# Weights' low halves: all of them on VectorE, in two pieces a slot

## The chip, the cores and the metric

The kernel runs on one core of a Trainium2 chip. The metric is the device time of one execution in microseconds (us), the median of several runs. Inputs, weights and outputs are in fp32 and lie in the chip's main memory.

## The reference

A trunk of two layers works on two requests of 256 positions with 1024 features, with shared weights. Cut to what matters:

```python
def trunk(x, ...):
    for l in range(DEPTH):                       # 2 layers
        h = rmsnorm(x, g_mix[l])
        u_a, v_a, q, k, v_b, g_a, g_b = split(h @ w_in[l])
        y_a = spatial_gating(u_a, v_a, sgu_g[l], sgu_w[l], sgu_b[l])
        y_b = diff_attention(q, k, v_b, lam, lam_init, rel_bias, sub_g[l])
        br = einsum('nbsc,ncd->nbsd', stack([y_a, y_b]), w_br[l])
        merged = sigmoid(g_a) * br[0] + sigmoid(g_b) * br[1]
        x = x + merged @ w_out[l]
        x = x + conv_gated_mlp(rmsnorm(x, g_ffn[l]), w_up[l], conv_w[l], conv_b[l], w_down[l])
    return rmsnorm(x, g_final)
```

diff_attention has 8 heads with two softmax maps each; conv_gated_mlp is an up-projection to 2 x 2816 columns, a depthwise convolution of width 3, a gelu gate and a down-projection. Nearly all arithmetic is in the products with the weight matrices.

## The kernel before

**Slots.** Both requests lie side by side as 512 columns. The weight matrices are worked through in blocks of 1024 rows x 256 columns ("slots"), 74 a layer: 16 of q, k, v and va (S_R), 4 of u (S_U), 16 of gates and branches (S_M1, S_M2), 4 of w_out (S_O), 22 of w_up (S_F), 12 of w_down (S_D; 8 of these have seven rows of tiles, not eight). Slot s uses buffer s % 2 of raw, w_hi and w_lo. SyncE loads raw; ScalarE writes the high half w_hi as two copies, L480 for the first kd(s) of the eight tiles of 256 columns and L481 for the rest; the low half w_lo = raw - w_hi comes in two pieces too, the first from VectorE (L837, waits for the first copy), the rest from GpSimd (L416, waits for the second). kd(s) is 4 in slots 0 to 3, 1 in slots 4 to 19, 3 elsewhere, so the rest has 1024, 1792 or 1280 elements a partition (1024 where a slot has seven tiles). TensorE makes each product from three matmuls a tile, high x high (L1188), low x high (L1189) and high x low (L1190), for two halves of 128 columns; in the v and va slots these are L1223 to L1225. SyncE loads slot s+2 when both pieces of slot s are done.

**Queues.** Every engine's program is written out by hand and done in that order; semaphores tie the engines together. hi_split counts ScalarE's copies, lo_vector and lo_pool the pieces of w_lo.

**Attention rounds.** The projections of q, k, v, va and u are interleaved with the heads' attention in four rounds (r = 0 to 3) of eight steps (i = 0 to 7), two heads a round, one query tile a step. In step i TensorE does half a slot, then the values product of the tile two steps back (L1274, into the one bank HEAD), the transposition of attn of the last step, and the logits of two steps ahead (L1247). VectorE in step i: split of the coming slot if i is even; softmax_out (reciprocal L898, map_ratio L900, attn L905); at i = 6 and, from round 1 on, i = 2 head_scale (L911 and head_o L915), which empties the bank HEAD after a head's four tiles; at i = 0 and 4 head_lo (yb_lo L921); softmax_in of the next tile (L886, L890); at i = 1 to 4 the low parts of the next heads' q and k (L847); and the evacuation of TensorE's half slot (L864, L874 or L961). ScalarE in step i: squares of the head, at even i the two copies of the slot (L480, L481), the high parts of q or k (L547, L549), head_hi (L589), the transposed attn (L566), the exponentials (L556). GpSimd does half of the low parts of k (L426) beside its w_lo pieces, and the sums of squares of the norms (L401, L404).

The head values product must wait for head_o when it starts a new head:

```python
                if a % 4 == 0 and a:
                    pe.wait_ge(head_o_ok, l * HEADS + a // 4)
```

**After the rounds** spatial_gating (L968 on) works a 256-column block at a time: a split, the gates, another split, mix (L991, L998), ya_lo (L1002) and, once, the last head's yb_lo; the last head's branch product is L1373 to L1375. In the MLP, mlp(i) copies the conv parameters (L1054), splits two slots, evacuates four half slots (L1063) and convolves each (ScalarE L706, VectorE L1069 and L1072).

## Time and profile before

| | |
|---|---|
| median of 3 runs | 1741.06 us (1739.48 to 1742.98) |
| the profiled execution | 1740.8 us |
| its span, first to last instruction | 1738.8 us |
| TensorE's mean granted clock | 0.996 of full speed |
| TensorE busy | 98% of the span |
| VectorE, ScalarE, GpSimd busy | 55%, 43%, 33% |
| memory traffic | 101 GB/s on average |

The profile's page has busy times, a picture of the span in 40 slices and the costliest groups. Behind it stand views of the trace: who waited for whom, groups of instructions by line and shape, and the instructions in order of time. In the order of time a row is start in us, duration in us, engine and line, operation, output and inputs with partitions x elements, count, and in brackets the idle time before it with what ended it. Rows that follow one another closely are merged with a count. Instructions of one engine overlap by some 0.08 us, so the next one starts a little before the last has ended.

### The profile page before, as it was taken

The numbers are of one execution on the slowest core, as the hardware profiler recorded it, in microseconds if no ns is written. First come the engines' busy times: TensorE is split into PE (matmuls) and PEld (weight loads), VectorE is DVE, ScalarE is ACT, GpSimd is POOL, SyncE is SP. The second block draws the span as 40 slices with busy tenths as digits, with TensorE's granted clock in tenths as the row PEclk, the third lists the DMA queues.
The fourth block names the chain that finished last, engine by engine and source line by source line (L and its number), as shares of the span: only waits on it lengthen the run. The fifth ranks groups of instructions, "written<-read, shape, count | busy, mean of one in ns | idle before, by whom it ended". The sixth has DMA issues, their size and how long they took to land.

```text
span 1738.8 us, 21578 instructions
## 1 busy us (share of the span) xinstructions
PE 1708.6 (98%) x7950; PEld 1425.5 (82%) x7950; DVE 948.5 (55%) x1328; ACT 739.1 (43%) x1312; POOL 575.3 (33%) x216
## 2 busy tenths in 40 slices
PE   7999999999999999999999999999999999999997
PEld 5888888788888888888888888878888888888886
DVE  5677754543337777741147667545333477777122
ACT  5465654222344444432245656442223444443223
POOL 2544432322243222223344334223223432222332
PEclk8999999999999999999999999999999999999999
DMA  6422222222422222233253222322242232222332
GB/s 218 134 90 80 73 73 97 97 83 87 145 97 97 96 96 96 96 99 102 91 193 97 74 73 73 116 79 73 97 145 97 94 100 96 96 96 91 99 101 84
DMA packets 152303, 174.90 MB, mean 101 GB/s; under 512 B 2936, under 2 KB 141874, under 8 KB 151730
## 3 DMA queue, kind: packets, MB, share of 16 engines
q1 hardware_dynamic: 151328, 173.55, 30.2%
q10 hardware_dynamic: 914, 0.55, 0.2%
q8 instruction: 37, 0.61, 0.2%
q14 instruction: 24, 0.20, 0.0%
HBM read 167.78 MB, written 6.31 MB: 100 GB/s over the span
## 4 chain that ended last, share of the span: by engine, by line
PE 91%; DVE 5%; ACT 2%; issue 1%; ACTq 0%; DMA 0%; DVEq 0%
PE bank L1188 26%; PE bank L1190 26%; PE bank L1189 26%; PE bank L1223 3%; PE bank L1224 3%; PE bank L1225 3%; PE bank L1247 1%; PE bank L1274 1%; DVE attn L905 1%; DVE q_st L847 1%; PE bank L1346 1%; PE bank L1258 1%; DVE w_lo L837 0%; DMA table<-in_rel_bias 0%; DVE k_lo L847 0%
## 5 line engine op out<-in xcount | busy, mean ns | idle before, releaser
L416 POOL TENSOR_TENSOR w_lo<-raw,w_hi 128x1280 fp32r<-128x1280 f32 (+2 forms) x148 | 483.7, 3268 | 1085.0 <-ACT w_hi L481 1084.9
L1188 PE MATMUL bank<-xg_hi,w_hi 128*128 128x512 f32 x1344 | 527.2, 392 | 0.9 <-issue 0.9
L1190 PE MATMUL bank<-xg_hi,w_lo 128*128 128x512 f32 x1344 | 523.6, 390 | 0.0
L1189 PE MATMUL bank<-xg_lo,w_hi 128*128 128x512 f32 x1344 | 523.5, 390 | 0.0
L1188 PEld LDWEIGHTS bank<-xg_hi,w_hi 128*128 128x128 f32 x1344 | 252.8, 188 | 52.9 <-issue 2.3
L1190 PEld LDWEIGHTS bank<-xg_hi,w_lo 128*128 128x128 f32 x1344 | 252.6, 188 | 53.1
L1189 PEld LDWEIGHTS bank<-xg_lo,w_hi 128*128 128x128 f32 x1344 | 252.8, 188 | 51.9 <-issue 1.0
L837 DVE TENSOR_TENSOR w_lo<-raw,w_hi 128x768 fp32r<-128x768 f32 (+2 forms) x148 | 129.5, 875 | 193.5 <-ACT w_hi L480 193.3
L481 ACT ACTIVATE w_hi<-raw 128x1280 fp32r<-128x1280 f32 (+2 forms) x149 | 196.0, 1315 | 0.0
L480 ACT ACTIVATE w_hi<-raw 128x768 fp32r<-128x768 f32 (+2 forms) x149 | 112.5, 755 | 154.6 <-PE bank L1190 141.5
L1190 PE MATMUL bank<-g_hi,w_lo 128*128 128x512 f32 x352 | 136.9, 389 | 0.0
L1188 PE MATMUL bank<-g_hi,w_hi 128*128 128x512 f32 x352 | 136.9, 389 | 0.0
L1189 PE MATMUL bank<-g_lo,w_hi 128*128 128x512 f32 x352 | 136.9, 389 | 0.0
L706 ACT ACTIVATE conv<-up,conv_par 128x512 f32<-128x512 f32 x88 | 71.9, 817 | 146.8 <-DVE up L1063 146.8
L556 ACT ACTIVATE logit<-logit,neg_max 128x256 f32<-128x256 f32 x128 | 64.1, 502 | 128.7 <-DVE neg_max L890 128.4
L1063 DVE TENSOR_TENSOR up<-bank,rms 128x512 f32<-128x512 f32 x88 | 60.5, 687 | 75.0 <-PE bank L1190 56.0
L1223 PE MATMUL bank<-w_hi,xg_hi 128*128 128x512 f32 x256 | 100.4, 392 | 0.0
L1225 PE MATMUL bank<-w_lo,xg_hi 128*128 128x512 f32 x256 | 99.7, 389 | 0.0
L1224 PE MATMUL bank<-w_hi,xg_lo 128*128 128x512 f32 x256 | 99.6, 389 | 0.0
L1069 DVE SCALAR_TENSOR_TENSOR conv<-up,conv_par,conv 128x510 f32<-128x510 f32 x88 | 70.5, 801 | 53.3 <-ACT conv L706 53.2
L1188 PEld LDWEIGHTS bank<-g_hi,w_hi 128*128 128x128 f32 x352 | 66.1, 188 | 13.8
L1189 PEld LDWEIGHTS bank<-g_lo,w_hi 128*128 128x128 f32 x352 | 66.1, 188 | 13.7
(157 smaller groups left out, 2372.7 us busy)
## 6 DMA issues: line engine op xcount, KB each, us to landing
raw<-in_w_in SPq DMA_DIRECT2D x57, 1024.0 KB, 5.1
raw<-in_w_up SPq DMA_DIRECT2D x44, 1024.0 KB, 5.0
raw<-in_w_br SPq DMA_DIRECT2D x16, 1024.0 KB, 5.1
raw<-in_w_down SPq DMA_DIRECT2D x16, 896.0 KB, 4.7
raw<-in_w_out SPq DMA_DIRECT2D x8, 1024.0 KB, 5.1
raw<-in_w_down SPq DMA_DIRECT2D x8, 1024.0 KB, 5.1
x_spill<-x_res SPq DMA_DIRECT2D x2, 2048.0 KB, 7.6
x_res<-x_spill SPq DMA_DIRECT2D x2, 2048.0 KB, 9.6
```

The source lines that it names most:

```text
L416: nc.gpsimd.tensor_tensor(w_lo[p_][:, kd(s):n, :], raw[p_][:, kd(s):n, :], f32(w_hi[p_][:, kd(s):n, :]), ALU.subtract).then_inc(lo_pool, 1)
L480: nc.scalar.activation(w_hi[s % 2][:, 0:kd(s), :], raw[s % 2][:, 0:kd(s), :], ACT.Copy).then_inc(hi_split, 1)
L481: nc.scalar.activation(w_hi[s % 2][:, kd(s):n, :], raw[s % 2][:, kd(s):n, :], ACT.Copy).then_inc(hi_split, 1)
L706: nc.scalar.activation(conv[half][:, :, :], up[half][:, :, :], ACT.Identity, bias=conv_par[:, 3, ab, half:half + 1], scale=conv_par[:, 1, ...
L837: nc.vector.tensor_tensor(w_lo[p_][:, 0:kd(s), :], raw[p_][:, 0:kd(s), :], f32(w_hi[p_][:, 0:kd(s), :]), ALU.subtract).then_inc(lo_vector, 1)
L1069: nc.vector.scalar_tensor_tensor(c[:, :, 1:SEQ], u[:, :, 0:SEQ - 1], conv_par[:, 0, ab, half:half + 1], c[:, :, 1:SEQ], ALU.mult, ALU.add) ...
L1188: nc.tensor.matmul(out, w_hi[w][:, k, cols], x_hi[:, a, :], start=first and k == 0, stop=False)
L1189: nc.tensor.matmul(out, w_hi[w][:, k, cols], x_lo[:, a, :], start=False, stop=False)
L1190: mm = nc.tensor.matmul(out, w_lo[w][:, k, cols], x_hi[:, a, :], start=False, stop=last and k == kt - 1)
L1223: nc.tensor.matmul(bank[t][:, :], xg_hi[:, a, cols], wide_hi[:, k, :], start=first, stop=False)
L1224: nc.tensor.matmul(bank[t][:, :], xg_lo[:, a, cols], wide_hi[:, k, :], start=False, stop=False)
L1225: mm = nc.tensor.matmul(bank[t][:, :], xg_hi[:, a, cols], wide_lo[:, k, :], start=False, stop=last)
```

## The change

GpSimd's pieces of w_lo go to VectorE: split on VectorE now issues the first piece, waits for ScalarE's second copy, and issues the rest. The semaphore lo_pool is called lo_rest. On GpSimd only the low parts of k and the sums of squares are left, and its loops over slots are gone. What is computed is the same, as is kd(s). The program of TensorE, ScalarE and SyncE is the same but for the semaphore's name.

```diff
@@ -225,7 +225,7 @@
     raw_in = [sem(f"raw_in{i}") for i in range(2)]
     hi_split = sem("hi_split")
     lo_vector = sem("lo_vector")
-    lo_pool = sem("lo_pool")
+    lo_rest = sem("lo_rest")
     proj_done = sem("proj_done")
     evacuated = sem("evacuated")
     xg_hi_ok, xg_lo_ok = sem("xg_hi_ok"), sem("xg_lo_ok")
...
@@ -305,7 +305,7 @@
             def load(s, src, off=0, n=8):
 
                 sp.wait_ge(lo_vector, l * SLOTS + off + (s + 1))
-                sp.wait_ge(lo_pool, l * SLOTS + off + (s + 1))
+                sp.wait_ge(lo_rest, l * SLOTS + off + (s + 1))
                 sp.dma_start(raw[s % 2][:, 0:n, :], src).then_inc(raw_in[s % 2], 16)
 
             def block_of(w, col, kt=(0, 8)):
...
@@ -405,17 +405,8 @@
                       .then_inc(sum_ok, 1)
                 yield m
 
-        pool.wait_ge(hi_split, 2)
-        nc.gpsimd.tensor_tensor(w_lo[0][:, kd(0):, :], raw[0][:, kd(0):, :], f32(w_hi[0][:, kd(0):, :]), ALU.subtract)\
-          .then_inc(lo_pool, 1)
 
         for l in range(DEPTH):
-            def split(s, off=0, n=8):
-                p_ = s % 2
-                pool.wait_ge(hi_split, 2 * (l * SLOTS + off) + 2 * (s + 1))
-                nc.gpsimd.tensor_tensor(w_lo[p_][:, kd(s):n, :], raw[p_][:, kd(s):n, :], f32(w_hi[p_][:, kd(s):n, :]),
-                                        ALU.subtract).then_inc(lo_pool, 1)
-
             def k_parts(p, half):
 
                 t, hi, lo = qk_f32[half], k_hi[(2 * p + half) % 3], k_lo[(2 * p + half) % 3]
@@ -427,36 +418,13 @@
                       .then_inc(k_lo_pool, 1)
                     pool.wait_ge(k_lo_pool, l * 16 + 4 * p + (2 * half + m + 1))
 
-            split(1)
             for p in range(PAIRS):
-                split(4 * p + 2)
-                k_parts(p, 0)
-                split(4 * p + 3)
-                k_parts(p, 1)
-                split(4 * p + 4)
-                split(4 * p + 5)
-            split(S_U + 2)
-            split(S_U + 3)
-            with pool.Fori(0, (S_O - S_M1) // 2) as t:
-                for n in range(2):
-                    split(S_M1 + n, off=2 * t)
+                for half in range(2):
+                    k_parts(p, half)
             sums = add_squares(2 * l + 1)
-            for n in range(PAIRS + 2):
-                split(S_O + n)
-                for _ in range((0, 0, 1, 2, 2, 2)[n]):
-                    next(sums)
-            with pool.Fori(1, FSLOT) as i:
-                for n in range(2):
-                    split(S_F + n, off=2 * i)
-            split(S_D)
-            sums = add_squares(2 * l + 2)
-            for j in range(PAIRS):
-                for c in range(len(DCH)):
-                    split(S_D + 3 * j + c + 1, n=DCH[(c + 1) % 3][1])
-                    if c == 0:
-                        for _ in range((0, 1, 2, 2)[j]):
-                            next(sums)
             for _m in sums:
+                pass
+            for _m in add_squares(2 * l + 2):
                 pass
 
 
@@ -796,6 +764,9 @@
                 ve.wait_ge(hi_split, 1)
                 nc.vector.tensor_tensor(w_lo[0][:, 0:kd(0), :], raw[0][:, 0:kd(0), :], f32(w_hi[0][:, 0:kd(0), :]),
                                         ALU.subtract).then_inc(lo_vector, 1)
+                ve.wait_ge(hi_split, 2)
+                nc.vector.tensor_tensor(w_lo[0][:, kd(0):, :], raw[0][:, kd(0):, :], f32(w_hi[0][:, kd(0):, :]),
+                                        ALU.subtract).then_inc(lo_rest, 1)
         for m in (KT - 2, KT - 1):
             keep_x(m).then_inc(evacuated, 1)
         for m in KEPT_LATE:
@@ -831,11 +802,14 @@
             nc.vector.tensor_copy(par[:, :], par_of_l)\
               .then_inc(par_ok, 1)
 
-            def split(s, off=0):
+            def split(s, off=0, n=8):
                 p_ = s % 2
                 ve.wait_ge(hi_split, 2 * (l * SLOTS + off) + (2 * s + 1))
                 nc.vector.tensor_tensor(w_lo[p_][:, 0:kd(s), :], raw[p_][:, 0:kd(s), :], f32(w_hi[p_][:, 0:kd(s), :]),
                                         ALU.subtract).then_inc(lo_vector, 1)
+                ve.wait_ge(hi_split, 2 * (l * SLOTS + off) + (2 * s + 2))
+                nc.vector.tensor_tensor(w_lo[p_][:, kd(s):n, :], raw[p_][:, kd(s):n, :], f32(w_hi[p_][:, kd(s):n, :]),
+                                        ALU.subtract).then_inc(lo_rest, 1)
 
             def qk_lo(p, o):
 
@@ -1110,7 +1084,7 @@
             for j in range(PAIRS):
                 for c in range(len(DCH)):
                     s = S_D + 3 * j + c
-                    split(s + 1)
+                    split(s + 1, n=DCH[(c + 1) % 3][1])
                 for half in range(2):
                     m = 2 * j + half
                     ve.wait_ge(proj_done, proj_n(l, S_D + 3 * j + 2, half))
@@ -1174,7 +1148,7 @@
             def split_ready(s, off=0):
                 pe.wait_ge(lo_vector, l * SLOTS + off + (s + 3))
             def split_ready_rest(s, off=0):
-                pe.wait_ge(lo_pool, l * SLOTS + off + (s + 3))
+                pe.wait_ge(lo_rest, l * SLOTS + off + (s + 3))
 
             def product(out, s, half, x_hi, x_lo, kt, k0=0, first=True, last=True, before_k=None, k_pool=None):
```

VectorE in step 2 of round 1, before: one w_lo piece of 256 elements, softmax_out, head_scale, softmax_in, q's low part, the evacuation.

```order
L837 TENSOR_TENSOR w_lo0_53<-raw0_49,w_hi0_51 128x256 [waits hi_split]
L898 RECIPROCAL map_inv_105<-exp_sum0_67 128x2 [waits exp_ok]
L900 SCALAR_TENSOR_TENSOR map_ratio0_106<-map_inv_105,par_59,exp_sum0_67 128x1 [waits recip_ok]
L905 SCALAR_TENSOR_TENSOR attn0_99<-logit0_97,map_ratio0_106 128x256 [waits trans_done,ratio_ok]
L911 TENSOR_TENSOR map_inv_105<-map_inv_105,head_rms_109 128x4 [waits head_rms_ok]
L915 TENSOR_TENSOR head_o_103<-bank7,map_inv_105 128x512 [waits head_t,head_wt_ok]
L886 SCALAR_TENSOR_TENSOR logit1_98<-bank5,bias_t_96 128x512 [waits qk_done]
L890 TENSOR_REDUCE neg_max1_66<-logit1_98 128x2 [waits biased]
L847 TENSOR_TENSOR q_st2_83<-qk_f32_1_91,q_st2_83 64x512 [waits qk_hi_ok]
L847 TENSOR_TENSOR q_st2_83<-qk_f32_1_91,q_st2_83 64x512
L864 TENSOR_TENSOR qk_f32_0_90<-bank2,rms_57 128x512 [waits qk_lo_vector,proj_done]
```

The same place now:

```order
L808 TENSOR_TENSOR w_lo0_53<-raw0_49,w_hi0_51 128x256 [waits hi_split]
L811 TENSOR_TENSOR w_lo0_53<-raw0_49,w_hi0_51 128x1792 [waits hi_split]
L872 RECIPROCAL map_inv_105<-exp_sum0_67 128x2 [waits exp_ok]
L874 SCALAR_TENSOR_TENSOR map_ratio0_106<-map_inv_105,par_59,exp_sum0_67 128x1 [waits recip_ok]
L879 SCALAR_TENSOR_TENSOR attn0_99<-logit0_97,map_ratio0_106 128x256 [waits trans_done,ratio_ok]
L885 TENSOR_TENSOR map_inv_105<-map_inv_105,head_rms_109 128x4 [waits head_rms_ok]
L889 TENSOR_TENSOR head_o_103<-bank7,map_inv_105 128x512 [waits head_t,head_wt_ok]
L860 SCALAR_TENSOR_TENSOR logit1_98<-bank5,bias_t_96 128x512 [waits qk_done]
L864 TENSOR_REDUCE neg_max1_66<-logit1_98 128x2 [waits biased]
L821 TENSOR_TENSOR q_st2_83<-qk_f32_1_91,q_st2_83 64x512 [waits qk_hi_ok]
L821 TENSOR_TENSOR q_st2_83<-qk_f32_1_91,q_st2_83 64x512
L838 TENSOR_TENSOR qk_f32_0_90<-bank2,rms_57 128x512 [waits qk_lo_vector,proj_done]
```

A second piece of 1792 elements, with a wait of its own for hi_split, stands ahead of everything else in the step.

GpSimd over the same rounds, before (slots' low halves w_lo between the low parts of k):

```order
L416 TENSOR_TENSOR w_lo0_53<-raw0_49,w_hi0_51 128x1792 [waits hi_split,k_lo_pool]
L416 TENSOR_TENSOR w_lo1_54<-raw1_50,w_hi1_52 128x1792 [waits hi_split]
L416 TENSOR_TENSOR w_lo0_53<-raw0_49,w_hi0_51 128x1792 [waits hi_split]
L426 TENSOR_TENSOR k_lo1_88<-qk_f32_0_90,k_hi1_85 64x512 [waits qk_hi_ok]
L426 TENSOR_TENSOR k_lo1_88<-qk_f32_0_90,k_hi1_85 64x512 [waits k_lo_pool]
L416 TENSOR_TENSOR w_lo1_54<-raw1_50,w_hi1_52 128x1792 [waits hi_split,k_lo_pool]
L426 TENSOR_TENSOR k_lo2_89<-qk_f32_1_91,k_hi2_86 64x512 [waits qk_hi_ok]
L426 TENSOR_TENSOR k_lo2_89<-qk_f32_1_91,k_hi2_86 64x512 [waits k_lo_pool]
```

Now:

```order
L417 TENSOR_TENSOR k_lo2_89<-qk_f32_0_90,k_hi2_86 64x512 [waits qk_hi_ok,k_lo_pool]
L417 TENSOR_TENSOR k_lo2_89<-qk_f32_0_90,k_hi2_86 64x512 [waits k_lo_pool]
L417 TENSOR_TENSOR k_lo0_87<-qk_f32_1_91,k_hi0_84 64x512 [waits qk_hi_ok,k_lo_pool]
L417 TENSOR_TENSOR k_lo0_87<-qk_f32_1_91,k_hi0_84 64x512 [waits k_lo_pool]
L417 TENSOR_TENSOR k_lo1_88<-qk_f32_0_90,k_hi1_85 64x512 [waits qk_hi_ok,k_lo_pool]
L417 TENSOR_TENSOR k_lo1_88<-qk_f32_0_90,k_hi1_85 64x512 [waits k_lo_pool]
```

Only the low parts of k are left, and nothing stands between them.

## Rows read from the trace of the kernel before

**Rows 1.** The page: busy us of each engine, share of the span, instructions.

```profile
PE 1708.6 (98%) x7950; PEld 1425.5 (82%) x7950; DVE 948.5 (55%) x1328; ACT 739.1 (43%) x1312; POOL 575.3 (33%) x216
```

**Rows 2.** Waits of TensorE: what for, us in total, times, longest.

```profile
PE bank L1373 <- DVE yb_lo L921: 3.9, 2, 2.0
PE bank L1247 <- DVE yb_lo L921: 2.8, 4, 1.6
...
PE bank L1274 <- DVE head_o L915: 2.1, 2, 1.1
PE bank L1188 <- issue: 0.9, 1, 0.9
```

**Rows 3.** Groups by line and shape, count | busy us, mean ns | idle before.

```profile
L837 DVE TENSOR_TENSOR w_lo<-raw,w_hi 128x768 fp32r<-128x768 f32 x108 | 103.0, 954 | 143.9 <-ACT w_hi L480 143.7
...
L1054 DVE COPY conv_par<-par 128x16 f32 x20 | 58.4, 2920 | 0.0
...
L416 POOL TENSOR_TENSOR w_lo<-raw,w_hi 128x1792 fp32r<-128x1792 f32 x32 | 130.1, 4065 | 212.5 <-ACT w_hi L481 212.5
```

**Rows 4.** Order of time, VectorE, steps 2 and 3 of round 1.

```profile
135.21 0.42 DVE L837 TENSOR_TENSOR w_lo<-raw,w_hi 128x256 fp32r<-128x256 f32 x1 [1.12 <-ACT w_hi L480]
135.55 0.16 DVE L898 RECIPROCAL map_inv<-exp_sum 128x2 f32<-128x2 f32 x1
...
136.60 0.69 DVE L915 TENSOR_TENSOR head_o<-bank,map_inv 128x512 f32<-128x512 f32 x1
...
138.64 3.52 DVE L847 TENSOR_TENSOR q_st<-qk_f,q_st 64x512 fp32r<-64x512 f32 x2
142.18 0.69 DVE L864 TENSOR_TENSOR qk_f<-bank,rms 128x512 f32<-128x512 f32 x1
```

**Rows 5.** Order of time, ScalarE, GpSimd and TensorE in the same steps.

```profile
135.08 1.69 ACT L481 ACTIVATE w_hi<-raw 128x1792 fp32r<-128x1792 f32 x1
...
136.85 4.05 POOL L416 TENSOR_TENSOR w_lo<-raw,w_hi 128x1792 fp32r<-128x1792 f32 x1 [10.15 <-ACT w_hi L481]
...
139.79 0.60 PE L1274 MATMUL bank<-v_tok,attn_t 128*128 128x128 f32 x4
...
145.37 0.36 ACT L566 ACTIVATE attn_t<-bank 128x256 f32<-128x256 f32 x1
```

**Rows 6.** Order of time, all engines, step 4 of round 1.

```profile
147.68 1.69 ACT L481 ACTIVATE w_hi<-raw 128x1792 fp32r<-128x1792 f32 x1
...
149.69 4.17 DVE L905 SCALAR_TENSOR_TENSOR attn<-logit,map_ratio 128x256 f32<-128x256 f32 x1
153.79 0.74 DVE L921 SCALAR_TENSOR_TENSOR yb_lo<-bank,par,yb_hi 128x512 fp32r<-128x512 f32 x1
...
154.67 0.36 PE L1247 MATMUL bank<-k_hi,q_st 128*128 128x256 f32 x1 [0.41 <-DVE yb_lo L921]
```

**Rows 7.** Order of time, step 6 of round 3.

```profile
272.13 1.26 ACT L481 ACTIVATE w_hi<-raw 128x1280 fp32r<-128x1280 f32 x1
...
276.80 0.69 DVE L915 TENSOR_TENSOR head_o<-bank,map_inv 128x512 f32<-128x512 f32 x1
...
277.64 0.68 PE L1274 MATMUL bank<-v_tok,attn_t 128*128 128x128 f32 x4 [1.07 <-DVE head_o L915]
```

**Rows 8.** Order of time, ahead of the last head's branch product.

```profile
303.41 1.26 ACT L481 ACTIVATE w_hi<-raw 128x1280 fp32r<-128x1280 f32 x1
...
305.61 3.24 DVE L998 TENSOR_TENSOR mix<-mix,u_t 128x512 f32<-128x512 f32 x2
```

**Rows 9.** Order of time, steps 1 to 3 of round 0.

```profile
76.45 1.76 DVE L900 SCALAR_TENSOR_TENSOR map_ratio<-map_inv,par,exp_sum 128x1 f32<-128x1 f32 x1
...
84.73 3.80 DVE L847 TENSOR_TENSOR q_st<-qk_f,q_st 64x512 fp32r<-64x512 f32 x2
...
91.75 0.36 ACT L566 ACTIVATE attn_t<-bank 128x256 f32<-128x256 f32 x1
...
93.21 0.60 PE L1274 MATMUL bank<-v_tok,attn_t 128*128 128x128 f32 x4
```

More of the change, by code:

```diff
@@ L318, in load_wide @@
                 sp.wait_ge(lo_vector, l * SLOTS + (s + 1))
-                sp.wait_ge(lo_pool, l * SLOTS + (s + 1))
+                sp.wait_ge(lo_rest, l * SLOTS + (s + 1))
                 v = w_in[bass.ds(l, 1)].rearrange("a (t p) c -> p (a t) c", p=P)
@@ L375, in _ @@
         sp.wait_ge(lo_vector, DEPTH * SLOTS + 1)
-        sp.wait_ge(lo_pool, DEPTH * SLOTS + 1)
+        sp.wait_ge(lo_rest, DEPTH * SLOTS + 1)
         sp.dma_start(raw[0][:, :, :], w_in[0, :, 0:CW].rearrange("(t p) c -> p t c", p=P)).then_inc(raw_in[0], 16)
@@ L393, in _ @@
                                 pattern=[[-1, P]], channel_multiplier=1).then_inc(ident_ok, 1)
-        nc.gpsimd.memset(junk[:, :], 0.0).then_inc(lo_pool, 2)
+        nc.gpsimd.memset(junk[:, :], 0.0).then_inc(lo_rest, 2)
         def add_squares(norm):
```

## The prediction

> **What bounds the kernel now.** I read the page's first part, then the waits of TensorE, then the order of time around each wait. TensorE is busy 1708.6 of 1738.8 us, VectorE 948.5 and GpSimd 575.3 [rows 1]. So shortening work on the other two buys nothing in itself: what can be won or lost is the time in which TensorE waits. Three of its waits are for VectorE: 3.9 us for the low half of a head's values (L1373, 2 times), 2.8 for the same inside the attention rounds (L1247, 4 times) and 2.1 for the scaled head output (L1274, 2 times), 8.8 us together [rows 2]. Outside the attention part and its end no wait for VectorE appears until the output. The question is what becomes of those 8.8 us, and which new waits come.
>
> **What is removed.** GpSimd loses all its pieces of the weights' low halves; in the attention rounds one took 4.065 us [rows 3]. VectorE instructions that read two SBUF operands stand still while such a piece runs: attn (L905) at 149.69 took 4.17 us and ended at 153.86 [rows 6], a pair of q_st took 3.52 us from 138.64 while GpSimd's piece ran to 136.85 + 4.05 = 140.90 [rows 4, 5], a copy of 16 elements of conv parameters took 2.92 us on average in 20 instances [rows 3], where a reciprocal of 2 elements takes 0.16 [rows 4], so some 2.75 of it is standing still. The Trainium skill, page "SBUF — State Buffer", section "Who interferes with whom", says that a Vector instruction with two SBUF inputs and a GpSimd instruction that reads SBUF exclude each other for the whole instruction, whoever came first; by that rule, with which the 4.17 us agree, the stalls of rows 6 end with the pieces, and without it 5.4 us of the sum below would not be won.
>
> **What is added.** VectorE gets 32 pieces of 1792 elements, 92 of 1280 and 24 of 1024. No such size runs there undisturbed in the rows shown. From 256 elements in 0.42 us [rows 4] to 768 in 0.954 [rows 3] is 1.04 ns an element, so 1792 take 2.02, 1280 1.49 and 1024 1.22 us, and what follows starts some 0.08 earlier. The bounds: 1.87 (1.04 ns times 1792 without any fixed part) and 4.065 (as slow as GpSimd). I take 2.02, since VectorE's rows are the near ones. Sum: 32 x 2.02 + 92 x 1.49 + 24 x 1.22 = 231 us of VectorE work, some 55 of it given back by the parameter copies alone (20 x 2.75).
>
> **The added wait.** The second piece waits for ScalarE's second copy (L481), and VectorE takes its work in order, so all that is queued behind the pieces now waits for that copy and for the piece itself.
>
> Step 2 of round 1 as the pattern: the first piece ran at 135.21, the reciprocal behind it at 135.55, head_o at 136.60 to 137.29 [rows 4]. ScalarE's second copy ended at 135.08 + 1.69 = 136.77 [rows 5]. New: second piece at 136.80, the reciprocal at 136.80 + 1.94 = 138.74 (3.19 later), head_o done at 138.74 + (137.29 - 135.55) = 140.48. TensorE needs it at 139.79 for the next values (L1274) [rows 5]; with the 0.15 us from head_o's end to TensorE's start that rows 7 let one work out (276.80 + 0.69 to 277.64, head_o of that place) it starts at 140.63: **0.84 us of new wait**. The same distances stand at step 6 of rounds 0, 1 and 2 and at step 2 of rounds 1, 2 and 3, six places a layer, twelve in all: 10.1 us (one of them has 0.25 us less room; left out).
>
> Step 6 of round 3 waits already, 1.07 us, because attn was blocked there [rows 7]. Its second copy ends at 272.13 + 1.26 = 273.39, the piece has 1280 elements: 273.42 + 1.41 + 1.74 = 276.57, TensorE could start at 276.57: 0.15 us stays, 0.3 in two layers.
>
> Step 3 of round 0: the transposed attn (L566) comes 3.19 us after the evacuation (L864) starts (145.37 - 142.18 [rows 4, 5]; and 91.75 against an evacuation 0.03 us behind the end of q_st at 88.53 [rows 9]). In round 0 step 0 hands on 3.19 us of lateness, less the 1.54 that a blocked L900 of 1.76 us gives back [rows 9]: 1.65. Step 2 adds its second piece behind ScalarE's later copy and loses 2.41 of q_st's 3.80 us (undisturbed pair 1.39, bounded by half of its 3.52 in rows 4): evacuation at 90.41 in place of 88.56, L566 ends at 90.41 + 3.19 + 0.36 = 93.96, TensorE starts values at 94.09 in place of 93.21 [rows 9]: 0.88 us, 1.8 in two layers. In the other rounds L566 has some 0.3 us left, since TensorE has just waited 0.84 itself.
>
> **What goes.** Step 4 of round 1: with ScalarE and VectorE 0.84 later, the second copy ends at 147.68 + 1.69 + 0.84 = 150.21 [rows 6], the piece at 152.26, attn and yb_lo follow, yb_lo ends at 154.15 at the latest. TensorE comes for it at 154.67 - 0.41 + 0.84 = 155.10 [rows 6]: the wait goes, and with it all 2.8 us of L1247. Of L1274 the 2.1 go (the 0.3 is counted above). Before L1373 the blocked pair L998 took 3.24 us from 305.61 and ended at 308.85; new: second copy ends at 304.67, piece 1.41, the two mixes 1.20, the pair 1.29: 308.6. So 0.25 of each wait goes, 0.5 in all [rows 8]. Removed: 2.8 + 2.1 + 0.5 = 5.4 us.
>
> **Where it costs nothing.** In the MLP loop a pair of slots gets 2 x 1.49 us and loses 2.75 at the parameter copy: 0.2 more in 21.8 us, and TensorE's waits show nothing there. TensorE needs a low half there only a slot later; without that cover each slot would cost 1.5. The branch, output-projection and down-projection slots have a half-idle VectorE and no wait in rows 2. GpSimd's sums of squares no longer queue behind weights, but nobody of TensorE waited for them. At the start TensorE waits 0.9 us (L1188) [rows 2], perhaps for the first weight piece that shared the port; the second slot's piece would be waited for instead, so I take 0 of it, with 0 and -0.9 as bounds.
>
> **Sum.** New waits 10.1 + 0.3 + 1.8 = 12.2, removed 5.4, net +6.8 us on the profiled run's 1740.8: 1747.6. The median of before lies 0.3 above that run, so I say **1747.9**.
>
> **Rivals.**
> (a) Faster: head_o is not late enough. The slack at the pattern place is 139.79 - 137.29 - 0.15 = 2.35 us against a lateness of 3.19. If the lateness stays below 2.35 (ScalarE's second copy overlapping the first piece by 0.84 more), the twelve new waits vanish, the 1.8 and 0.3 with them, and 5.4 is won: 1735.7. For it: GpSimd's idle 575 us and four kinds of blocked instructions. Against it: the copy's 1.69 us is in the row. The Trainium skill, "GPSIMD Engine Reference", section "Engine selection", says elementwise work belongs on VectorE, GpSimd being some two times slower; by that rule it comes out so.
> (b) Same: the lateness is some 0.4 us less than worked out, so half of the new waits stays: 6.1 against the 5.4 removed, +0.7, 1741.8. For it: the sum hangs on differences of a few tenths.
> (c) Much slower: the k_lo parts stay on GpSimd and now start as soon as k_hi is there. If they block one more VectorE instruction a round for 1.7 us, the 0.3 us left of L566 are eaten in the six other steps 3: 6 x 1.4 = 8.4 more, 1756.3. It decides from a lateness of 0.3 us on.
> (d) The blocked instructions were slow for another reason, so that the change doesn't free them: the 5.4 are not won, 1753.3. Rows 6 speak against it.
>
> **How the numbers follow.** Forecast (1744 to 1752) 0.58, (a) 0.12, (b) 0.15, (c) 0.08, (d) 0.07. One tenth of a microsecond in the piece or the copy moves 12 places, 1.2 us; a piece between 1.87 and 2.3 us gives -1.8 to +3.4, and one of 4.065, GpSimd's own, +25, which I leave out. The range that leaves out (a) and (c), 0.20, and takes in (b) and (d) is 1740 to 1755. A measurement can tell 0.2%, 3.5 us, from no change: faster 0.13 (a and a little of b), same 0.17 (the rest of b and the foot of the forecast), slower 0.70.
>
> **What would show it.** Right: VectorE near 1055 us busy, GpSimd near 90; q_st, attn and parameter copies at their short durations; TensorE's waits for head_o (L1274) 14 times, up to 0.9 each and some 10 us; two waits for ScalarE's L566 of 0.9; no wait at L1247; L1373 near 3.4. Wrong: fewer or no waits at L1274 (a, b); waits for ScalarE at step 3 of every round (c); long q_st or attn as before (d); any wait for weights in the MLP.

## The result

The changed kernel takes 1747.35 us (median of 7 runs, 1746.87 to 1748.37) against 1742.98 for the kernel before (7 runs, 1739.48 to 1743.72): a ratio of 1.0033, 95% interval 1.0022 to 1.0043. (That is not the quotient of the two medians, which is 1.0025.) It is slower, by about 0.3%, and the interval is clear of no change. The forecast was 1747.9, with a range from 1740 to 1755. The profiled execution took 1747.01 (span 1745.0), where that of the kernel before took 1740.8 (span 1738.8): 6.2 us more. The medians differ by less, 4.4 us, because the seven runs of the kernel before fall in two groups, two at 1739.5 to 1741.1 and five at 1742.9 to 1743.7, and its profiled execution lies with the first.

The page of the changed kernel, its part with the busy times, which answers to [rows 1]:

```profile
PE 1710.6 (98%) x7950; PEld 1423.6 (82%) x7950; DVE 1050.1 (60%) x1477; ACT 735.1 (42%) x1312; POOL 90.6 (5%) x67
```

GpSimd lost 485 us of work, VectorE got 102 more (231 us of pieces, less some 129 us by which its other instructions became shorter), and the kernel became slower. Why stands in the waits of TensorE (what for, us in total, times, longest), which answer to [rows 2]:

```profile
PE bank L1248 <- DVE head_o L889: 8.4, 12, 0.9
...
PE bank L1347 <- DVE yb_lo L895: 3.4, 2, 1.7
...
PE bank L1248 <- ACT attn_t L534: 1.3, 2, 0.6
PE bank L1162 <- DVE w_lo L808: 1.1, 1, 1.1
```

L1248 is the product with the values (L1274 before), L1347 the last head's branch product (L1373 before), L1162 a weight product. The waits for the low half yb_lo inside the rounds are gone, and twelve waits for head_o stand there that were not there before.

Groups of VectorE by line and shape (count | busy us, mean ns | idle before), which answer to [rows 3], the second pieces (L811) first:

```profile
L811 DVE TENSOR_TENSOR w_lo<-raw,w_hi 128x1280 fp32r<-128x1280 f32 x92 | 136.8, 1486 | 6.8 <-ACT w_hi L449 6.6
...
L811 DVE TENSOR_TENSOR w_lo<-raw,w_hi 128x1792 fp32r<-128x1792 f32 x32 | 64.8, 2024 | 29.0 <-ACT w_hi L449 29.0
...
L879 DVE SCALAR_TENSOR_TENSOR attn<-logit,map_ratio 128x256 f32<-128x256 f32 x64 | 31.0, 485 | 2.3
...
L811 DVE TENSOR_TENSOR w_lo<-raw,w_hi 128x1024 fp32r<-128x1024 f32 x24 | 29.2, 1219 | 0.0
...
L821 DVE TENSOR_TENSOR q_st<-qk_f,q_st 64x512 fp32r<-64x512 f32 x32 | 22.0, 687 | 3.7 <-ACT q_st L515 3.1
...
L1028 DVE COPY conv_par<-par 128x16 f32 x20 | 3.3, 167 | 0.0
```

The three shapes of the second piece cost 230.8 us. attn had a mean of 755 ns before and has 485, the copy of the conv parameters fell from 2920 to 167.

The pattern place, step 2 of round 1, in order of time; VectorE, then TensorE; it answers to [rows 4, 5]:

```profile
136.38 0.42 DVE L808 TENSOR_TENSOR w_lo<-raw,w_hi 128x256 fp32r<-128x256 f32 x1 [1.12 <-ACT w_hi L448]
137.97 2.02 DVE L811 TENSOR_TENSOR w_lo<-raw,w_hi 128x1792 fp32r<-128x1792 f32 x1 [1.17 <-ACT w_hi L449]
139.91 0.16 DVE L872 RECIPROCAL map_inv<-exp_sum 128x2 f32<-128x2 f32 x1
...
140.95 0.69 DVE L889 TENSOR_TENSOR head_o<-bank,map_inv 128x512 f32<-128x512 f32 x1
```

```profile
141.79 0.68 PE L1248 MATMUL bank<-v_tok,attn_t 128*128 128x128 f32 x4 [0.68 <-DVE head_o L889]
```

After its first piece VectorE stands for 1.17 us until ScalarE's second copy is done, then works 2.02 on the second piece; the reciprocal starts at 139.91, where it followed the first piece by 0.34 before (135.21 to 135.55 in [rows 4]), which would be 136.72 here: 3.19 us late, exactly the lateness of the forecast. TensorE is idle 0.68 us for it. (The reciprocal, L872, is the first instruction behind the pieces, and head_o stands four places behind it.)

### The profile page after: what moved, and what is told of

Same layout as the page of the kernel before. It is cut to its first block, busy times and chain, and to the rows that moved or that the text cites. A ratio compares the mean times of both kernels' runs of the same rounds, so it can differ in the third digit from the quotient of the medians.

```text
span 1745.0 us, 21498 instructions
## 1 busy us (share of the span) xinstructions
PE 1710.6 (98%) x7950; PEld 1423.6 (82%) x7950; DVE 1050.1 (60%) x1477; ACT 735.1 (42%) x1312; POOL 90.6 (5%) x67
## 4 chain that ended last, share of the span: by engine, by line
PE 85%; DVE 7%; ACT 5%; issue 2%; DMA 0%; ACTq 0%; DVEq 0%
PE bank L1162 24%; PE bank L1164 24%; PE bank L1163 24%; PE bank L1197 3%; PE bank L1199 3%; PE bank L1198 2%; DVE w_lo L811 2%; ACT w_hi L449 2%; PE bank L1248 2%; PE bank L1221 1%; ACT logit L524 1%; PE bank L1320 1%; DVE head_o L889 1%; PE bank L1232 1%; DVE logit L860 0%
## 5 line engine op out<-in xcount | busy, mean ns | idle before, releaser
L1162 PE MATMUL bank<-xg_hi,w_hi 128*128 128x512 f32 x1344 | 526.5, 392 | 1.1 <-DVE w_lo L808 1.1
L1162 PEld LDWEIGHTS bank<-xg_hi,w_hi 128*128 128x128 f32 x1344 | 252.5, 188 | 53.7 <-DVE w_lo L808 1.9
L811 DVE TENSOR_TENSOR w_lo<-raw,w_hi 128x1280 fp32r<-128x1280 f32 (+2 forms) x148 | 230.8, 1559 | 35.9 <-ACT w_hi L449 35.6
L808 DVE TENSOR_TENSOR w_lo<-raw,w_hi 128x768 fp32r<-128x768 f32 (+2 forms) x148 | 136.5, 922 | 179.9 <-ACT w_hi L448 179.7
L1162 PE MATMUL bank<-g_hi,w_hi 128*128 128x512 f32 x352 | 136.9, 389 | 0.0
L1043 DVE SCALAR_TENSOR_TENSOR conv<-up,conv_par,conv 128x510 f32<-128x510 f32 x88 | 66.0, 750 | 53.9 <-ACT conv L674 53.7
L1162 PEld LDWEIGHTS bank<-g_hi,w_hi 128*128 128x128 f32 x352 | 66.1, 188 | 13.7
```

Of the source, the lines that this page charges most:

```text
L808: nc.vector.tensor_tensor(w_lo[p_][:, 0:kd(s), :], raw[p_][:, 0:kd(s), :], f32(w_hi[p_][:, 0:kd(s), :]), ALU.subtract).then_inc(lo_vector, 1)
L811: nc.vector.tensor_tensor(w_lo[p_][:, kd(s):n, :], raw[p_][:, kd(s):n, :], f32(w_hi[p_][:, kd(s):n, :]), ALU.subtract).then_inc(lo_rest, 1)
L1162: nc.tensor.matmul(out, w_hi[w][:, k, cols], x_hi[:, a, :], start=first and k == 0, stop=False)
```

## The experiments

### Is it head_o behind the piece?

**Twelve waits, taken away by a shorter piece.** In the second piece's line, for slots 4 to 19:

```diff
+                n = kd(s) + 1 if 4 <= s < S_M1 else n
                 nc.vector.tensor_tensor(w_lo[p_][:, kd(s):n, :], raw[p_][:, kd(s):n, :], f32(w_hi[p_][:, kd(s):n, :]),
                                         ALU.subtract).then_inc(lo_rest, 1)
```

> The changed kernel, but in slots 4 to 19 of each layer (those loaded in the attention rounds) VectorE's second piece computes one tile of 256 elements only, so the low half of the other six tiles is left out there. The piece still waits for ScalarE's second copy, and is some 1.6 us shorter. Theory (head_o is late because it stands behind the piece, 3.19 us late against 2.35 of room): lateness falls to 1.6, so the twelve waits for head_o (0.68 us each in the trace of the changed kernel, 0.93 with the restart) and the two for the transposed attn of 0.65 go: 12 x 0.93 + 2 x 0.9 = 13 us less than the changed kernel, about 1734, 0.995 of the kernel before. Rival A (the wait for ScalarE's second copy makes it late, not the piece's own time): the waits stay above 0.5 and the time above 1744. Rival B (TensorE waits there for another reason, head_o being only the last signal): no change, 1747.

"The restart" is what TensorE loses around a stop beside the idle time that the view shows, some 0.25 us; the part on the prediction works it out.

Measured: 1733.96 us (4 runs), 0.9957 of before, interval 0.994 to 0.9974. TensorE's waits, all that are left behind the first weight product:

```profile
PE bank L1348 <- DVE yb_lo L896: 3.4, 2, 1.7
...
PE bank L1412 <- DVE y_tok L1100: 0.9, 1, 0.9
PE bank L1163 <- DVE w_lo L808: 0.9, 1, 0.9
```

All fourteen waits went, and 13.4 us with them, where 13 were expected. The wait for ScalarE's second copy is still in this kernel, so it alone is not enough to make head_o late: rival A falls, and so does B. The piece alone, without that wait, would by the same sum not be enough either (1.94 us of lateness against 2.35 of room); that is an estimate, and no run here leaves out the wait and keeps the place.

**The piece twice.** For slots 4 to 19 the second piece is computed once more ahead of itself:

```diff
+                if 4 <= s < S_M1:
+                    nc.vector.tensor_tensor(w_lo[p_][:, kd(s):n, :], raw[p_][:, kd(s):n, :], f32(w_hi[p_][:, kd(s):n, :]),
+                                            ALU.subtract).then_inc(twice, 1)
+                    n_twice[0] += 1
+                    ve.wait_ge(twice, n_twice[0])
```

> The changed kernel, but VectorE computes its second piece twice in slots 4 to 19 of each layer, some 2.1 us more of VectorE a slot. Theory: each of the twelve waits for head_o grows one for one, from 0.68 to some 2.7 us (+25 us), the two for the transposed attn by 2 to 4 each (+4 to +8), and where nothing waited (step 4 of rounds 0 to 2, the low half of the head's values) some 1.1 us appear in up to six places (+7). Together 1783 to 1788. Rival B (head_o is not what holds TensorE): under 10 us more.

Measured: 1833.99 us (one run), 86.6 more than the changed kernel. The direction was right and the size missed by a factor of two. TensorE's waits:

```profile
PE bank L1255 <- DVE head_o L896: 36.2, 12, 4.0
PE bank L1228 <- DVE yb_lo L902: 18.2, 12, 2.8
PE bank L1255 <- ACT attn_t L536: 9.0, 4, 2.9
```

These three come to 63.4 us where the changed kernel has 9.7: 53.7 more. The logits' wait for yb_lo came in twelve places, not six. The other 33 us go with the clock. Its windows (us, busy us and instructions of each engine, granted clock, DMA share, GB/s) and TensorE in order of time behind the wait at 226.02:

```profile
210.00:220.00 10.00, 9.73 (x50) 8.36 (x51) 6.66 (x13) 6.94 (x19) 0.00 (x0) 1.00 0.29 104
220.00:230.00 10.00, 7.01 (x28) 5.81 (x27) 9.53 (x15) 3.71 (x11) 0.00 (x0) 0.77 0.32 105
```

```profile
226.02 1.19 PE L1255 MATMUL bank<-v_tok,attn_t 128*128 128x128 f32 x4 [2.99 <-DVE head_o L896]
...
228.72 0.63 PE L1170 MATMUL bank<-xg_lo,w_hi 128*128 128x512 f32 x1
...
232.13 0.42 PE L1169 MATMUL bank<-xg_hi,w_hi 128*128 128x512 f32 x1
232.39 0.39 PE L1170 MATMUL bank<-xg_lo,w_hi 128*128 128x512 f32 x1
```

After 2.99 us of idling, matmuls of 512 columns took 0.63 us and not 0.39 until 232: the 1.2 GHz level in place of 2.4. The mean granted clock is 0.978, in the changed kernel 0.997; (0.997 - 0.978) x 1831 = 35 us, an estimate that is a little above the 33 that are left. So a long wait costs a second time, and the waits of 0.68 us of the changed kernel do not: its windows through the rounds have a granted clock of 1.00.

### Do GpSimd's pieces hold VectorE up?

**Short pieces on GpSimd.** Two kernels, each the kernel before with one line more in GpSimd's `split`: the first has the first of the two added lines, the second the other, and takes slot 20 (S_M1) out of its loop:

```diff
                 pool.wait_ge(hi_split, 2 * (l * SLOTS + off) + 2 * (s + 1))
+                n = kd(s) + 1 if 4 <= s < S_M1 else n
+                n = kd(s) + 1 if 4 <= s <= S_M1 and isinstance(off, int) else n
```

> The kernel before, but in slots 4 to 19 of each layer GpSimd's piece computes one tile of 256 elements only (the low half of the other six tiles is left out there), so GpSimd works some 0.7 us a slot in place of 4.07. Theory (VectorE instructions that read two SBUF operands stand still while GpSimd's piece runs): attn, q_st and k_lo of the attention rounds fall to their short durations (0.49, 0.69 and some 1.06 us), TensorE's waits for yb_lo inside the rounds (2.8 us in 4) and for head_o (2.1 in 2) go, the one for the last head's low half stays (slot 20 is whole): 4.9 + 6 x 0.25 = 6.4 us less than before, 0.9963. Rival (they are slow for another reason): durations and waits as before, 1.000.

> The kernel before with GpSimd's piece cut to one tile of 256 elements in slots 4 to 20 of each layer (the low half of the other tiles is left out there): the run with slots 4 to 19 cut, and slot 20 in addition. Theory (TensorE's wait of 1.07 us for head_o at step 6 of round 3 stands there because slot 20's piece blocks attn): that wait goes in both layers, 2.1 us by the view, some 2.6 with the restart: 1738.5 - 2.6 = 1735.9, 0.9963 of before. Rival (it has another cause): as the run without slot 20, 0.9978.

Measured: 1738.49 us (10 runs), 0.9978, interval 0.9969 to 0.9988, with slots 4 to 19 cut; 1736.3 (5 runs), 0.9964, interval 0.995 to 0.9978, with slot 20 as well. VectorE's groups between 60 and 315 us of the first of them:

```profile
L906 DVE SCALAR_TENSOR_TENSOR attn<-logit,map_ratio 128x256 f32<-128x256 f32 x32 | 18.1, 567 | 1.1
L848 DVE TENSOR_TENSOR k_lo<-qk_f,k_hi 64x512 fp32r<-64x512 f32 x12 | 12.2, 1019 | 3.0 <-ACT k_hi L550 2.9
L848 DVE TENSOR_TENSOR q_st<-qk_f,q_st 64x512 fp32r<-64x512 f32 x12 | 8.2, 687 | 0.3
```

and TensorE's waits for VectorE in it:

```profile
PE bank L1374 <- DVE yb_lo L922: 3.9, 2, 2.0
...
PE bank L1275 <- DVE head_o L916: 2.1, 2, 1.1
```

In the same stretch of the kernel before, attn has a mean of 712 ns, k_lo 1184 and q_st 1242. With GpSimd's work shortened and nothing else touched they fall to 567, 1019 and 687, and the 2.8 us of waits for yb_lo inside the rounds are gone. The wait of 1.07 us at step 6 of round 3 stayed in the first kernel, against my expectation of 6.4 us, and went in the second, which differs in slot 20 alone: no wait for head_o is in its list. Its ratio of 0.9964 is what the first was expected to give (0.9963); by the medians it gained 5.1 us. So GpSimd's piece is what blocked these instructions, place by place, and rival (d) falls. The Trainium skill, page "SBUF — State Buffer", section "Who interferes with whom", says that a Vector instruction with two SBUF inputs and a GpSimd instruction that reads SBUF exclude each other; these runs agree (q_st 1242 against 687 ns). It counts a copy in one of VectorE's two-port modes among the instructions that contend; the trace of the changed kernel agrees with the parameter copies at 167 ns in place of 2920, though it doesn't show in which mode a copy ran. (The prediction listed these copies among the instructions with two SBUF operands; a copy reads only one.)

### Where does the difference lie?

**Attention rounds alone, and all but the attention rounds.** Two mirror kernels. A rule says by slot who computes the second piece, and each waits on its own count:

```diff
+def on_vector(s):
+
+    return (4 <= s % SLOTS < S_M1) == True
...
+                if on_vector(s):
+                    ve.wait_ge(hi_split, 2 * (l * SLOTS + off) + (2 * s + 2))
+                    nc.vector.tensor_tensor(w_lo[p_][:, kd(s):n, :], raw[p_][:, kd(s):n, :], f32(w_hi[p_][:, kd(s):n, :]),
+                                            ALU.subtract).then_inc(lo_rest, 1)
```

> Only slots 4 to 19 of each layer as in the changed kernel (VectorE does both pieces); GpSimd keeps its pieces of all other slots. Nothing is left out. Theory (the whole difference lies in the attention rounds): the same twelve waits for head_o of 0.68 and two of 0.65 for the transposed attn, none for yb_lo inside the rounds, 1.95 in 2 ahead of the last head's product as before: +13.0 - 6.4 = 6.6 us more than before, 1.0038, a little above the changed kernel's 1.0033. Rival (GpSimd's absence outside the rounds gives or costs something): this differs from the changed kernel by more than 2 us.

> The mirror of the last one: VectorE does both pieces in all slots but 4 to 19 of each layer, where GpSimd keeps its piece. Nothing is left out. Theory: the waits of the rounds are those of the kernel before (yb_lo 2.8 us in 4, head_o 2.1 in 2), no wait for head_o of 0.68; the last head's 3.9 become 3.4, and the start gives 0.4 to 0.7: 1 us less than before, 0.9994. Rival (the 124 pieces outside the rounds cost VectorE time that TensorE feels, in the loops above all): 1.001 or more.

Measured: rounds only, 1752.43 us (4 runs), 1.0061 (1.0044 to 1.0078); outside only, 1737.74 (10 runs), 0.9975 (0.9966 to 0.9984). TensorE's waits for the other engines, of the first and of the second:

```profile
PE bank L1302 <- DVE head_o L940: 10.5, 14, 1.1
...
PE bank L1401 <- DVE yb_lo L946: 3.9, 2, 2.0
...
PE bank L1302 <- ACT attn_t L587: 1.3, 2, 0.7
PE bank L1216 <- issue: 1.2, 1, 1.2
```

```profile
PE bank L1395 <- DVE yb_lo L940: 3.4, 2, 1.7
PE bank L1269 <- DVE yb_lo L940: 2.9, 4, 1.6
```

The parts add up, as well as the runs can tell: by the medians +10.1 and -4.7 us against before give +5.4, where the whole change gives +4.4; by the ratios it is +6.3 against +5.7. The rounds cost more than the whole change, and the rest of the program gives something back.

I had both sizes wrong, in part by the same thing: the wait at step 6 of round 3 hangs on slot 20, which is outside the slots 4 to 19. It stays in the first kernel (14 waits, not 12) and goes in the second. The time from the first to the last values product of the rounds, both layers together, shows its price: 428.2 us in the first kernel against 426.2 in the changed one, 2.0 more; 416.9 in the second against 418.7 in the kernel before, 1.8 less.

That leaves 1.5 us of the 3.5 between expectation and measurement in the first, and 1.9 of the 3.7 in the second. The traces show two things that bear on it. One is the clock behind the wait of 1.95 us at the last head, which comes below. The other is the start: the first values product starts at 85.60 in the second kernel and at 86.62 in the kernel before.

**The start alone.** The kernel before with the second half of slot 0 of layer 0 on VectorE, and the changed kernel with it on GpSimd. The edit of the first:

```diff
-        pool.wait_ge(hi_split, 2)
-        nc.gpsimd.tensor_tensor(w_lo[0][:, kd(0):, :], raw[0][:, kd(0):, :], f32(w_hi[0][:, kd(0):, :]), ALU.subtract)\
-          .then_inc(lo_pool, 1)
...
+                ve.wait_ge(hi_split, 2)
+                nc.vector.tensor_tensor(w_lo[0][:, kd(0):, :], raw[0][:, kd(0):, :], f32(w_hi[0][:, kd(0):, :]),
+                                        ALU.subtract).then_inc(lo_first, 1)
```

> The kernel before, but the second half of the very first slot's low half (slot 0 of layer 0) on VectorE as in the changed kernel; everything else stays on GpSimd. Nothing is left out. In the traces so far VectorE's first piece there took 2.09 us beside GpSimd's and 1.20 without, TensorE's first product started at 20.68 against 19.57, and its matmuls reached the full pitch at 23.80 (in another kernel with GpSimd's piece at about 25.5) against 20.56 and 22.7 without it. Theory (the start gains the earlier product and the earlier clock, less what slot 1 then waits for its transfer): TensorE's wait ahead of the first product goes, the mean granted clock rises from 0.994 to 0.996, 1.5 to 2.5 us less than before, 0.9988. Prediction's value: 0 to 0.9 less. Everything from slot 1 on as before. Rival (what the kernels without GpSimd's pieces win at the start comes from elsewhere, or slot 1's wait takes all of it): 1.000.

> The mirror: the changed kernel, with GpSimd doing the second half of slot 0 of layer 0 as in the kernel before. Nothing is left out. Theory: TensorE waits some 1 us ahead of its first product, slot 1's wait of 1.1 us goes, the mean granted clock falls to 0.994: 1.5 to 2.5 us more than the changed kernel's 1747.35, about 1749.5, 1.0043 of before. Rival: unchanged, 1747.

Measured: 1740.15 us (11 runs), 0.9997 (0.9987 to 1.0006), and 1748.02 (6 runs), 1.0035 (1.0022 to 1.0047). VectorE's first piece and TensorE's first products, with VectorE doing both halves, then with GpSimd beside it:

```profile
17.97 1.20 DVE L799 TENSOR_TENSOR w_lo<-raw,w_hi 128x1024 fp32r<-128x1024 f32 x1
19.11 1.20 DVE L802 TENSOR_TENSOR w_lo<-raw,w_hi 128x1024 fp32r<-128x1024 f32 x1
```

```profile
19.28 0.77 PE L1196 MATMUL bank<-xg_hi,w_hi 128*128 128x512 f32 x1
...
22.74 0.39 PE L1198 MATMUL bank<-xg_hi,w_lo 128*128 128x512 f32 x1
```

```profile
18.41 1.98 DVE L773 TENSOR_TENSOR w_lo<-raw,w_hi 128x1024 fp32r<-128x1024 f32 x1
```

```profile
20.49 0.77 PE L1170 MATMUL bank<-xg_hi,w_hi 128*128 128x512 f32 x1 [0.83 <-issue]
...
25.30 0.40 PE L1172 MATMUL bank<-xg_hi,w_lo 128*128 128x512 f32 x1
```

The mechanism is plain in the traces: beside GpSimd's piece VectorE's first piece takes 1.98 us and not 1.20, TensorE starts its first product 1.2 us later, after standing idle, and its matmuls reach the full pitch 2.6 us later (25.30 against 22.74). What it is worth at the end is less plain. The runs of the kernel before fall in two groups, in this series 7 of 15 between 1740.0 and 1741.0 (granted clock 0.996 and above) and 8 between 1741.4 and 1743.2 (mostly 0.994); with slot 0 on VectorE 7 of 11 lie between 1739.8 and 1740.4 and the other 4 between 1741.4 and 1741.8. The medians differ by 1.2 us and the interval holds no change; the mirror kernel by 0.7 in the other direction, from another series.

The traces tell more than the medians. In the seven kernels with both halves of slot 0 on VectorE (all but the doubled one, which waits earlier) the first values product of the rounds starts between 85.2 and 86.3 us, in the five with GpSimd's half between 86.6 and 87.2: 1.1 us apart on average. From there on the trace with slot 0 on VectorE is that of the kernel before, stretch by stretch, to 0.1 us. So the start is worth about 1 us, below the expected 1.5 to 2.5.

**What makes the two groups.** The start doesn't: they are still there with slot 0 on VectorE. Two groups, 1.6 to 2.4 us apart, show in the kernel before, in the one with slot 0 on VectorE and in both with short pieces on GpSimd. These, and the one with the rounds alone changed, have the wait of 1.95 us ahead of the last head's product. In three of the ten such waits in their traces the granted clock fell right behind it. The short pieces, slots 4 to 19, layer 1:

```profile
1157.28 0.50 PE L1374 MATMUL bank<-yb_hi,w_hi 128*128 128x512 f32 x1 [1.95 <-DVE yb_lo L922]
...
1158.37 0.63 PE L1374 MATMUL bank<-yb_hi,w_hi 128*128 128x512 f32 x1
...
1161.27 0.40 PE L1190 MATMUL bank<-xg_lo,w_hi 128*128 128x512 f32 x1
```

From the last values product to the end of the span it is 593.7 us there and 592.1 in the kernel before, whose profiled execution has no such fall: 1.6 us. The kernel with the rounds alone changed has the same 1.6 us in its trace, which is part of its +10.1. In the seven traces with a wait of 1.69 us in that place, the changed kernel's among them, the clock never fell, and apart from one execution of the mirror kernel their times lie within 2 us of one another, kernel by kernel. So the changed kernel also avoids a risk that the kernel before runs. That the upper group of the kernel before is this fall is likely, and not shown: no execution of that group has a trace, and 1.6 us is not the whole distance of its groups, 2.0 us between their means.

### Is it the load or the order?

**The same pieces, later in the step.** The second piece gets a function of its own, `split_rest`, which is called later; the first call goes ahead of the evacuation of the step, the second kernel has it behind:

```diff
                     if i % 2 == 0:
-                        split(4 * (r + 1) + i // 2 + 1)
+                        split_first(4 * (r + 1) + i // 2 + 1)
                     softmax_out(r, i)
...
+                    if i % 2 == 0:
+                        split_rest(4 * (r + 1) + i // 2 + 1)
                     if r + 1 < PAIRS:
```

> The changed kernel, with the second piece in slots 5 to 20 issued on VectorE behind the step's attn, head_o and the next logits, ahead of the evacuation, in place of ahead of them all. Nothing is left out and nothing is shorter. Theory: the twelve waits for head_o go (8.4 us by the trace, 11.2 with the restart); the evacuation comes as late as in the changed kernel, so the two waits for the transposed attn stay: 1747.3 - 11.2 = 1736, 0.9968 of before. Rival (VectorE's load, not its order, makes the waits): they return elsewhere, above 1744.

> As the one before, but the second piece stands at the end of its step, behind the evacuation too. Theory: the evacuation is some 2 us earlier, so the two waits for the transposed attn go as well: 1747.3 - 11.2 - 1.8 = 1734.3, 0.9957 of before; the wait of 3.4 us in 2 ahead of the last head's product stays. Rival: attn of the next step, now behind the piece, is late and TensorE waits for its transpose in odd steps: up to 0.5 x 16 more, 1742.

Measured: 1733.59 us (5 runs), 0.9951 (0.9937 to 0.9965), and 1733.89 (5 runs), 0.9952 (0.9938 to 0.9965). No wait for head_o or for the transposed attn is left in either. Step 2 of round 1 of the second of them:

```profile
134.86 0.43 DVE L812 TENSOR_TENSOR w_lo<-raw,w_hi 128x256 fp32r<-128x256 f32 x1 [1.12 <-ACT w_hi L448]
135.20 0.16 DVE L879 RECIPROCAL map_inv<-exp_sum 128x2 f32<-128x2 f32 x1
...
136.24 0.69 DVE L896 TENSOR_TENSOR head_o<-bank,map_inv 128x512 f32<-128x512 f32 x1
...
139.70 0.69 DVE L845 TENSOR_TENSOR qk_f<-bank,rms 128x512 f32<-128x512 f32 x1
140.31 2.02 DVE L818 TENSOR_TENSOR w_lo<-raw,w_hi 128x1792 fp32r<-128x1792 f32 x1
```

The same 2.02 us of work is there, but head_o ends at 136.93 and TensorE wants it at 139.44; the wait for ScalarE's second copy is gone too, as the copy is long done when the piece's turn comes. The load did no harm, the order did. (Slots 5 to 20 are what moves here; slot 4 and the slots outside the rounds have the order of the changed kernel.) In the first kernel I expected the waits for the transposed attn to stay; they went. The evacuation of step 2 of round 0 starts at 86.40 in place of 89.73; 0.7 us of that is the start of the program (slot 1 begins at 32.49 and not 33.21), the rest comes from VectorE's not standing 0.59 us for ScalarE's copy there and from the steps before, which hand on less lateness. I had left both out.

**And at the last head.** In addition the second piece of slot 22 goes behind the last head's low half:

```diff
+                (split_first if last_head else split)(S_M1 + 2, off=2 * j)
...
                     head_lo(HEADS - 1)
+                    split_rest(S_M1 + 2, off=2 * j)
```

> As the one before, and the second piece of slot 22, which stands ahead of the mix and the low half of the last head (yb_lo), goes behind that low half. Theory: the wait of 1.69 us in each layer shrinks by the piece's 1.41 and the wait for ScalarE's second copy, to 0.2 at most: 3.3 us less again, 1731.0, 0.9938 of before. Rival (the two products before the low half, waiting for ScalarE's mix, set it): 1 us less at most.

Measured: 1730.13 us (5 runs), 0.9932, interval 0.9918 to 0.9945: 12.3 us below the kernel before and the fastest of all. TensorE's waits, whole but for those of its first transposes for transfers:

```profile
PE bank L1148 <- DVE par_all L737: 3.4, 1, 3.4
...
PE bank L1421 <- DVE y_tok L1109: 0.9, 1, 0.9
...
PE bank L1172 <- DVE w_lo L812: 0.3, 1, 0.3
```

The wait of 1.7 us in each layer went whole, and 3.8 us with the two: yb_lo is done at 304.73 (303.98 + 0.75), TensorE comes for it at 304.78, and the view has no wait of TensorE between slot 1 and the output.

## Why the prediction was right

The mechanism was right: the kernel is slower because head_o stands behind the second piece in VectorE's queue, at the places named. The number came closer than the difference did. Forecast was +6.8 us on a kernel before of 1741.1; measured was +6.2 between the profiled executions and +4.4 between the medians, with 1743.0 for the kernel before. That 1747.9 and 1747.35 lie only 0.6 apart is in part luck: the three runs that the forecast stood on had a lower median, and three of its terms were off in ways that nearly cancel.

**The pattern place held to the hundredth.** Lateness 3.19 forecast, 3.19 measured. TensorE was to start the values 0.84 us later. In the kernel with the piece last, where nothing waits, they start 6.59 us after those of the step before (132.85 to 139.44); in the changed kernel it is 7.42 (134.37 to 141.79), 0.83 more. The view calls only 0.68 of it idle: in a run of matmuls the next starts 0.23 us after the one before (279.45 and 279.68, say), whose own row is 0.39 long, and the idle time counts from that row's end, 0.16 later. What the sum left out comes behind: the first group behind the wait takes 0.68 and not 0.60, and the next step's values are some 0.1 us later again. From the values of step 6 of round 0 to those of step 2 of round 1 it is 26.82 us where nothing waits (112.62 to 139.44) and 27.75 in the changed kernel (114.04 to 141.79). That is 0.93 a place, 11.2 us in twelve, where the sum had 10.1.

**Number and places.** Twelve waits for head_o at the forecast places: right. Step 6 of round 3 was to keep 0.15 us: head_o ends at 280.06 and TensorE starts at 280.21, which the list of waits doesn't count. But the values start 6.89 us after those of the step before there (273.32 to 280.21) and not 6.59, and the next ones another 0.08 later: 0.4 us a layer, 0.8 in both, where 0.3 was forecast. Two waits for the transposed attn in round 0: right, 0.65 each by the view and some 0.9 with the restart, against 0.88.

**What goes.** No wait at the logits (L1221 now), L1347 at 3.4 us, as forecast; the short pieces on GpSimd show the cause of those in the rounds. Here too the restarts were left out: the six waits that went were worth 4.9 + 6 x 0.25, some 6.4 us and not 4.9. So the prediction's new waits and its removed ones were both too small, and the errors nearly cancel.

**The start** was the term with the wrong value. I took 0 and gave 0.9 us as the most. Up to the first values product the changed kernel is 0.7 us ahead in the profiled execution: an earlier first product, a slow-clock stretch that is shorter (full pitch at 20.56 against 23.80) and then 1.10 us of wait for slot 1's first piece. I had seen the 0.9 us of idle time (L1188) and not that VectorE's own first piece was blocked there (2.09 us against 1.20), nor the clock behind it.

**The sum once more, from the two traces.** The starts of the values products cut the profiled executions into stretches (us):

| stretch | before | changed | difference |
|---|---|---|---|
| to the first values product (86.62, 85.94) | 86.6 | 85.9 | -0.7 |
| rounds of layer 0 (to 296.60, 299.18) | 210.0 | 213.2 | +3.3 |
| between the rounds (to 937.96, 940.24) | 641.4 | 641.1 | -0.3 |
| rounds of layer 1 (to 1146.69, 1153.20) | 208.7 | 213.0 | +4.2 |
| to the end of the span | 592.1 | 591.8 | -0.3 |

The rounds take 206.2 us a layer in the kernel with the piece last (86.27 to 292.43). So the new waits of the changed kernel cost 7.1 and 6.8 us, 13.9 together, where the forecast had 12.2; those of the kernel before cost 3.8 and 2.6, 6.4 together, where it had 4.9. 13.9 less 6.4, less 0.6 at the last head (0.5 forecast), less 0.7 at the start (0 forecast) is +6.2, all of the difference.

**VectorE's load:** 231 us forecast, 230.8 measured, 1050 busy against 1055; GpSimd 90.6 against 90. No wait in the MLP loop, as forecast.

**The rivals.** (a), faster, needed head_o less than 2.35 us late; it was 3.19, and the run with the short piece shows that below it the kernel does become faster (0.9957). The Trainium skill, "GPSIMD Engine Reference", section "Engine selection", has elementwise work on VectorE; the trace agrees on the price (4.065 us against 2.024 for 1792 elements), the result does not follow from it, as the order decided, and with the order mended it does (0.9952, and 0.9932 with slot 22 moved as well). (b) needed a lateness some 0.4 us smaller, and with it half the price of the new waits; it was 3.19, and they cost more than forecast, not less. (c) needed the transposed attn late in every round; it was late in round 0 alone. (d) fell with the short pieces on GpSimd.

## What to carry to other kernels

When work moves to an engine that runs its queue in order, its place in the queue matters more than its length: ask first what stands behind it that the bounding engine will want, and put it behind that. The some 65 us of second pieces in the attention rounds cost nothing where they stood behind head_o, and 13 us where they stood ahead of it. What to look for is an operand with little room: here 2.35 us of room stood against 3.19 of lateness. A wait costs its idle time and some 0.25 us around it, so count places, not only lengths.

## What the runs showed of the hardware

- **A stop of TensorE costs more than the view's idle time:** 0.93 us of time for 0.68 us of idling, at a regular place with the clock granted in full.
- **Longer stops cost the clock as well.** Behind waits of 0.68 us (1.7 at the last head) the granted clock stayed at 1.00. Behind ten waits of 1.95 us it fell to the 1.2 GHz level three times, at a price of 1.6 us each. Behind one of 2.99 us, matmuls ran at the 1.2 GHz level until 232.1, 6 us on, and an execution with 28 waits, up to 4.0 us long, had a mean of 0.978. The doubled piece cost 53.7 us in waits and some 33 more, which the mean clock accounts for (35 by the estimate above).
- **GpSimd's piece holds VectorE up.** Beside pieces of 4.07 us the low part of q took 1242 ns on average between 60 and 315 us, and 687 with the pieces shortened; a copy of 16 elements took 2920 ns and 167 without the pieces.
